# Key/query projection and attention in one block: value projection units inside the first page steps, prompt units merged to 24 in steps 9 to 32

## What is computed

```
kv = rmsnorm(h, kv_norm_w) @ w_kv            # after layer 0: keys, then values, 1024 columns each
q  = rmsnorm(h, norm_mix_w[1]) @ b_w_q       # 8 heads x (2 halves of 64)
# prompt, per head and block of 128 queries, c = 0, 1:
s = einsum(q_c, k_c) * 64**-0.5 - slope * dist      # causal
a = softmax(s[0]) - lam * softmax(s[1]);  o = a @ v
# sample, per sequence: the same over 16 cached pages (through page_table) and the 4 new tokens
def page_step(carry, p):
    kp, vp = cache_k[page_table[:, p]], cache_v[page_table[:, p]]
    s = einsum(qs, kp) + alibi;  return merge(carry, s, vp)
mix = rmsnorm(o, b_subln_w) * (1 - lam_init) @ b_w_o;  h = h + mix;  h = h + hier_moe(rmsnorm(h))
```

## Time and profile before

| | us |
|---|---|
| median of 3 executions | 1745.8 |
| lowest, highest | 1740.0, 1747.0 |
| the profiled execution, whole | 1740.4 |
| its span, first to last instruction | 1738.7 |
| TensorE busy in the span | 1364.6 (78%) |
| VectorE busy | 757.1 (44%) |
| ScalarE busy | 388.2 (22%) |
| bytes moved by DMA | 347.6 MB, 200 GB/s on average |

### The profile page before, as it was taken

The page is one execution under the profiler, slowest core; times in us unless marked ns, Lnnn a source line. Parts: engine busy times, 40 slices in busy tenths (PEclk is TensorE's granted clock), DMA queues, the critical chain, the costliest instruction groups (busy, mean ns, idle before and its releaser), DMA issues. The chain is left out here.

```text
span 1738.7 us, 29140 instructions
## 1 busy us (share of the span) xinstructions
PE 1364.6 (78%) x11207; PEld 790.7 (45%) x11207; DVE 757.1 (44%) x1922; ACT 388.2 (22%) x1062; POOL 170.9 (10%) x242
## 2 busy tenths in 40 slices
PE   3998888887599998908998946666677669999890
PEld 2445555554455655504444434434444325665450
DVE  4205555446665311132101167677777336531115
ACT  2013343333211111102001023333333211021111
POOL 1002222223101000020000011000000000100002
PEclk9998999998699899958998968888888779899995
DMA  5130334113343899830221079999999872589934
GB/s 197 49 127 22 109 105 141 53 61 109 100 174 134 309 371 346 274 122 17 97 100 49 8 236 363 356 367 376 366 357 357 328 244 110 197 299 354 354 101 158
DMA packets 132156, 347.56 MB, mean 200 GB/s; under 512 B 22012, under 2 KB 51887, under 8 KB 123824
## 3 DMA queue, kind: packets, MB, share of 16 engines
q1 hardware_dynamic: 115652, 315.21, 50.4%
q0 software_dynamic: 4992, 17.83, 2.9%
q10 hardware_dynamic: 11372, 12.62, 2.3%
HBM read 302.09 MB, written 43.52 MB: 199 GB/s over the span
## 5 line engine op out<-in xcount | busy, mean ns | idle before, releaser
L404 PE MATMUL bank<-wring,xT 128*128 128x512 f32 x512 | 239.3, 629 | 24.0 <-ACT gla_fin L527 16.1
L2285 DVE STREAM_TRANSPOSE wring<-wring 128x1024 f32<-128x1024 f32 x128 | 154.1, 1225 | 55.4 <-DMA wring<-cache_k 53.8
L404 PEld LDWEIGHTS bank<-wring,xT 128*128 128x128 f32 x512 | 102.0, 202 | 154.2 <-issue 132.9
L2175 PE MATMUL bank<-wring,sa_q 128*32 128x128 f32 x2048 | 89.7, 348 | 100.8 <-DVE sa_red L2294 93.7
L2175 PEld LDWEIGHTS bank<-wring,sa_q 128*32 128x32 f32 x2048 | 78.9, 142 | 110.0 <-issue 100.4
L1304 PE MATMUL bank<-wring,xT 128*128 128x512 f32 x256 | 119.4, 620 | 2.0 <-DVE xT L1224 2.0
L774 PE MATMUL bank<-xT,wring 128*128 128x512 f32 x256 | 111.9, 595 | 0.0
L1304 PEld LDWEIGHTS bank<-wring,xT 128*128 128x128 f32 x256 | 49.3, 199 | 59.4 <-issue 59.3
L682 DVE COPY_PREDICATED gla_att<-level_masks,bank 128x512 f32<-128x512 int32 x48 | 35.0, 730 | 92.6 <-PE bank L794 92.6
L774 PEld LDWEIGHTS bank<-xT,wring 128*128 128x128 f32 x256 | 48.1, 190 | 59.3 <-issue 59.3
L794 PE MATMUL bank<-gla_qe,gla_ke 128*128 128x128 f32 x384 | 52.8, 296 | 4.7 <-DVE gla_att L682 4.7
(11 more groups left out here) (420 smaller groups left out, 2259.3 us busy)
## 6 DMA issues: line engine op xcount, KB each, us to landing
wring<-cache_k SPq DMA_DIRECT2D x128, 512.0 KB, 5.7
wring<-cache_v SPq DMA_DIRECT2D x64, 512.0 KB, 7.3
xT<-cache_v SPq DMA_DIRECT2D x64, 512.0 KB, 6.1
moe_wd<-moe_w_down SPq DMA_DIRECT2D x20, 1024.0 KB, 13.4
wring<-moe_w_gate SPq DMA_DIRECT2D x18, 1024.0 KB, 11.1
wring<-moe_w_up SPq DMA_DIRECT2D x18, 1024.0 KB, 14.2
wring<-a_w_in SPq DMA_DIRECT2D x16, 1024.0 KB, 9.1
moe_wgu<-moe_w_gate SPq DMA_DIRECT2D x14, 1024.0 KB, 10.8
```

The lines of the kernel that those rows point to most:

```text
L404: last = nc.tensor.matmul(bank[:, :], xT[:, c, cols(t)], w[:, c, :], start=(c == 0), stop=(c == DC - 1))
L2175: last = nc.tensor.matmul(out.rearrange("p (r x) -> p r x", r=GROUP), Q[b % 2][:, h, i, :], keys.K[s % 2][:, :, at:at + QUAD], start=(i == ...
L2285: nc.vector.transpose(page, page).then_inc(keys_turned, 1)
```

## The change

1. The two blocks become one. The class Projections holds the instructions of the old projection block without the values; attention_block calls it at the start of each engine's stream. The turning of the keys, one head at a time, now follows each query unit, and the spread of the sample queries follows the third.
2. The ten value units run inside the page steps: two small ones and one large in slot -1, then one large in each of the slots 0 to 6, behind the step's score (value_units_at, V_UNITS). ScalarE copies them out (value_out), where VectorE did.
3. The page buffers change. Keys use a ring tile and the tile that held attn_q_xT. The value pages of the steps 0 to 2 (V_EARLY = 3) share one place, the tile that held the keys (attn_k), since xT and the weights are needed until the last value unit; from step 3 on values have two places as before. K(0) and K(1) are loaded when the queries are done.
4. Prompt units are 24: of each head the blocks 0 and 1 together, then 2, then 3. They start at slot 9 (FIRST = 9). Their tiles lie in the attn_k tile behind the early value pages, so that the table of distances (const_dist) is loaded, and v_prompt stored, in slot 8, when value(2) is done.
5. The load of b_w_o moves from slot 33 to behind the last value pages.
6. In MixOut.tensor, in both layers, gather(0) goes in between the halves of the last projection unit, and gather(2) ahead of norm_turn of the last tile.

```diff
@@ MixOut.tensor
             if i:
                 logits(i - 1)
+            if i == NT - 1:
+                gather(0)
             project(i, 1, w[1], second)
         place(NT - 2)
-        gather(0)
         gather(1)
+        gather(2)
         norm_turn(NT - 1)
         logits(NT - 1)
-        gather(2)
         gather(3)
         place(NT - 1)
@@ CachePages
-        self.K = [by_page(ring[0]), by_page(ring[1])]
-        spare = self.k.xT[:, :, :].rearrange("p c n -> p (c n)")[:, 0:GROUP * D]
-        self.V = [by_page(ring[2]), spare.rearrange("p (r n) -> p r n", r=GROUP)]
+        self.K = [ring[0], by_page(spare)]
+        self.V = [ring[2], by_page(self.k.xT[:, :, :].rearrange("p c n -> p (c n)"))]
+        self.V_early = by_page(early)
+    def values(self, s):
+        return self.V_early if s < V_EARLY else self.V[s % 2]
@@ Projections (was kvq_block)
+    def tensor(self, pe):
...
+        for h in range(HEADS):
+            if h < 2:
+                sample_q(h, w[h])
...
+            last.then_inc(self.q_done, 1)
...
+            turn_k(h)
+            if h == 2:
+                pe.wait_ge(self.qs_out, 2)
+                queries.spread_over_quarters((k.ps[0], k.ps[1]))
+        pe.wait_ge(self.kt_out, 2 * HEADS)
+        queries.new_scores(pe, k.ps[7])
+    def value_unit(self, pe, n):
...
+        if n >= 2:
+            pe.wait_ge(self.v_out, n - 1)
+        project_tokens(self.nc, bank, self.kv_xT, self.w[i], t).then_inc(self.v_done, 1)
+    def value_out(self, act, n):
+        i, t = V_UNITS[n]
+        act.wait_ge(self.v_done, n + 1)
+        for src, part in token_parts(self.k.ps[4 + n % 2], self.v, i, t):
+            last = self.nc.scalar.activation(part, src, ACT.Copy)
+        last.then_inc(self.v_out, 1)
+    def sync(self, sp):
...
+        sp.wait_ge(self.q_done, HEADS)
+        for s in range(2):
+            for r in range(GROUP):
+                keys.load_k(sp, s, r)
+V_UNITS = [(0, PT), (1, PT)] + [(i, t) for i in range(2) for t in range(PT)]
+V_FIRST, V_EARLY = 3, 3
-UNITS = [(h, i) for h in range(HEADS) for i in range(PT)]
-FIRST = 0
+UNITS = [(h, blocks) for h in range(HEADS) for blocks in ((0, 1), (2,), (3,))]
+FIRST = 9
+def value_units_at(s):
+    return range(V_FIRST) if s == -1 else range(V_FIRST + s, min(V_FIRST + s + 1, len(V_UNITS)))
@@ attention_block, SyncE (new order)
+                proj.sync(sp)
+                for s in range(STEPS + LAG):
+                    if 2 <= s < STEPS:
+                        sp.wait_ge(scored, s - 1)
+                        for r in range(GROUP):
+                            keys.load_k(sp, s, r)
...
+                    if s == 2:
...
+                            keys.load_v(sp, 0, r)
+                    v_s = s - LAG
+                    if v_s >= 1:
+                        if v_s >= V_EARLY:
+                            sp.wait_ge(proj.v_done, len(V_UNITS))
+                        if v_s < V_EARLY or v_s >= V_EARLY + 2:
+                            sp.wait_ge(valued, v_s if v_s < V_EARLY else v_s - 1)
+                        for r in range(GROUP):
+                            keys.load_v(sp, v_s, r)
...
+                    if v_s == V_EARLY:
+                        sp.wait_ge(valued, V_EARLY)
+                        sp.dma_start(dist[:, :], a["const_dist"]).then_inc(d_in, 16)
+                        sp.wait_ge(proj.v_out, len(V_UNITS))
+                        proj.store(sp, v, "v_prompt", None, proj.v_stored)
+                sp.wait_ge(scored, STEPS)
+                for i in range(2):
+                    k.load_weights(sp, column_halves(a["b_w_o"][0], i * HB))
@@ attention_block, TensorE and ScalarE
                     if 0 <= s < STEPS:
                         score(s)
+                    for n in value_units_at(s):
+                        proj.value_unit(pe, n)
...
+                    for n in value_units_at(s):
+                        proj.value_out(act, n)
                     if ends is not None:
                         exps(ends)
                         shift_exp(ends)
```

More of the change, by code:

```diff
@@ L1769, in __init__ @@
         self.S_new = sb("scores_new", [P, DEC_B, 2, DEC_T])
-        self.qs, self.kTs = sb("qs", [P, HEADS, SMP]), sb("kTs", [P, HEADS, SMP])
-        self.qz = sb("q_halves", [P, DEC_B, HEADS, QX])
+        n = HEADS * SMP
+        self.qs, self.kTs = (early[:, i * n:(i + 1) * n].rearrange("p (h t) -> p h t", h=HEADS) for i in range(2))
+        self.qz = early[:, 2 * n:4 * n].rearrange("p (b h x) -> p b h x", b=DEC_B, h=HEADS)
         self.rep = sb("q_rep", [P, GROUPS_, HEADS, SMP])
@@ L1857, in __init__, with place @@
         self.v_in = [k.sem(f"sa_v_landed{i}") for i in range(2 * GROUP)]
-    def place(self):
-        by_page = lambda tile: tile[:, :, :].rearrange("p (r c) n -> p r (c n)", r=GROUP)
-        ring = [self.k.wring[(self.k.w_issued + i) % WEIGHT_SLOTS] for i in range(WEIGHT_SLOTS)]
-        self.K = [by_page(ring[0]), by_page(ring[1])]
-        spare = self.k.xT[:, :, :].rearrange("p c n -> p (c n)")[:, 0:GROUP * D]
-        self.V = [by_page(ring[2]), spare.rearrange("p (r n) -> p r n", r=GROUP)]
+    def place(self, spare, early):
+        by_page = lambda flat: flat[:, 0:GROUP * D].rearrange("p (r n) -> p r n", r=GROUP)
+        ring = [by_page(self.k.wring[(self.k.w_issued + i) % WEIGHT_SLOTS][:, :, :].rearrange("p c n -> p (c n)"))
+                for i in range(WEIGHT_SLOTS)]
+        self.K = [ring[0], by_page(spare)]
[3 more added lines that the diff above has]
+        return self.V_early if s < V_EARLY else self.V[s % 2]
     def page(self, sp, s, r):
@@ L2033, in units_at, with parts_of @@
+V_UNITS = [(0, PT), (1, PT)] + [(i, t) for i in range(2) for t in range(PT)]
[4 more added lines that the diff above has]
+    return range(V_FIRST) if s == -1 else range(V_FIRST + s, min(V_FIRST + s + 1, len(V_UNITS)))
+def parts_of(n):
+    h, blocks = UNITS[n]
+    at = 0
+    for x, i in enumerate(blocks):
+        yield x, i, at, (i + 1) * P
+        at = at + (i + 1) * P
 def units_at(s):
@@ L2036, in units_at, with attention_block @@
     return (n,) if 0 <= n < len(UNITS) else ()
-def attention_block(k, a, rep, v, kT, qT, o_s, queries, keys):
+def attention_block(k, a, rep, v, kT, qT, o_s, S, queries, keys, proj):
     nc = k.nc
@@ L2125, in _ @@
                 p_bias_of(1)
-                for b in range(2, DEC_B):
+                for b in range(3, DEC_B):
                     spread_q(b)
-                    p_bias_of(b)
+                    p_bias_of(b - 1)
+                p_bias_of(DEC_B - 1)
                 k.order_n["gpsimd"] = ch.n
@@ L2147, in p_turn @@
                         pe.wait_ge(p_at_out, n)
-                    for j in range(i + 1):
+                    for j in range(sum(i + 1 for i in UNITS[n][1])):
                         last = nc.tensor.transpose(P_TURNED[:, j * P:(j + 1) * P], PS[n % NS][:, 0, j * P:(j + 1) * P], k.ident[:, :])
@@ L2156, in p_values @@
                         pe.wait_ge(p_o_out, n)
-                    for j in range(i + 1):
-                        last = nc.tensor.matmul(P_VALUE[:, 0:P], aT[:, j, :], v[:, j, h * P:(h + 1) * P],
-                                                start=(j == 0), stop=(j == i))
+                    for x, i, at, w in parts_of(n):
+                        for j in range(i + 1):
+                            last = nc.tensor.matmul(P_VALUE[:, x * P:(x + 1) * P], aT[:, at // P + j, :], v[:, j, h * P:(h + 1) * P],
+                                                    start=(j == 0), stop=(j == i))
                     last.then_inc(p_o_done, 1)
@@ L2208, in value @@
                             p = g * GROUP + r
-                            last = nc.tensor.matmul(VALUE[n][QUAD * r:QUAD * (r + 1), :], AT[:, p, :], keys.V[v_s % 2][:, r, n * HB:(n + 1) * HB],
+                            last = nc.tensor.matmul(VALUE[n][QUAD * r:QUAD * (r + 1), :], AT[:, p, :], keys.values(v_s)[:, r, n * HB:(n + 1) * HB],
                                                     start=(g == 0), stop=(g == GROUPS_ - 1 and r > 0))
@@ L2268, in p_bias_max @@
+                        last.then_inc(p_biased, 1)
                     dve.wait_ge(p_biased, 2 * (n + 1))
[L2269 removed]
+                    y = slice(0, len(blocks))
+                    nc.vector.tensor_scalar(s[:, y, 2:4], s[:, y, 0:2], -1.0, None, ALU.mult).then_inc(p_negated, 1)
                 def p_combine(n):
[L2272 to L2274 removed]
@@ L2282, in turn_page @@
+                    last.then_inc(p_combined, 1)
                 def turn_page(s, r):
```

399 lines of the change are left out of this document (186 added, 213 removed).

## The result

The changed kernel takes 1717.9 us (median of 4, 1714.0 to 1718.9), the kernel before beside it 1746.4 us (1740.0 to 1752.4): a ratio of 0.984, 95% interval 0.981 to 0.987. The change gains 28.5 us where 50 were forecast, and the time is 4 us above the end of the range (1714). In the two profiled executions the spans are 1738.7 and 1717.1 us, 21.6 us apart; the profiled execution of before is the shortest of its four.

The account below looks back on a forecast made before the run. TensorE bounds the value projection and the page stream the page steps, one after the other. Terms -52 + 6.5 + 3 - 4.5 - 3.2 = -50.2 us, against the median 1745.8, give 1696 us; range 1681 to 1714.

Parts of the forecast that it names:

- the sum of the start: Up to the issue of K(8): K(8) near 1025 instead of 1077.1, a gain of 52 us (bounds 42 and 60).
- the signs that the prediction named as wrong: Slots 0-6 above 10 us; even score waiting on ScalarE; step over 12 us behind slot 9; K(8) after 1035.
- Rival (a): Start: DMA runs dry, scores of steps 7 and 8 wait, 11.5 to 17 us lost, 1707 to 1713; chance 0.17.
- the softmax wait: Slot 4: TensorE's turn_weights waits for the softmax behind the value unit, 7 us (bounds 0 and 9).
- the 3 that were added: Slot 5, behind slot 4's wait: score and part of a unit at the low clock, 3 us.
- K(8) to K(31): Page stream: 6.5 us for the value store and const_dist plus 3 us for the prompt units' loop.
- The store: Value store (2.1 MB), now in the full page stream: 5.8 us at the stream's rate.
- rival (c): Page stream: prompt units' longer chain, VectorE waiting for ScalarE's exponentials, takes over the loop; 1746 or slower, say 1757; chance 0.02.
- the tail: After K(31): moving b_w_o behind V(31) removes value(28)'s page wait, -4.5 us (bounds -8 and 0).
- the routing: Moved gathers, both layers: last tile's choice 1.6 us earlier each, -3.2 us in all (bounds -7 and +4).
- Rival (b): Page stream gets faster: gaps at DMA share 0.95 filled, 5% of 265 us, 13 us won, 1683; chance 0.10.
- a rule's price: Start: by the skill's clock rule, slots with idle gaps would pay the value unit nearly twice.

Follow-up runs that it names:

- either link: Two runs against the changed kernel: K(7), K(8) issued ahead of V(1), V(2) on SyncE, 1703.0 us; bias_max(2) ahead of step 7's first transpose on VectorE, 1706.8 us.

## Where the prediction was right, and where not

**Wrong: the sum of the start**, by 20.8 of 52 us. The step that failed is the one that gives slot 6 the same 8.9 us as the slots before it, and lets only V(2) wait for the early place. V(1) waits for it too, and it stands ahead of K(7) in SyncE's order. In TensorE's timeline the 20.8 us are score(6)'s wait, 13.3; the low clock of that score and its unit, 3.64 + 7.77 - 1.93 - 7.13 = 2.3; a wait of 2.1 before score(2), which the sum did not have either, with 1.7 for the low clock behind it; and 1.4 in small pieces, the largest 1.1 between the end of value(1) and K(8)'s issue. Of the signs that the prediction named as wrong, two came: slots above 10 us (slot 2 took 12.7, slot 6 24.6) and K(8) after 1035. Cutting either link brought K(8) to 1016.7 and 1027.8, on both sides of the 1025 forecast.

**Rival (a) had the mechanism and a chance of 0.17.** It named the scores of steps 7 and 8; it was score(6), through VectorE's order. Its argument against, that V lands 6 to 7 us behind its issue, took the landing of a first page (6.3 us in the earlier trace rows); a value step needs all four pages, 8.7 us behind the first issue for V(2), 1037.9 to 1046.6. And it counted one landing; the chain has value(0), an issue of V, an issue and a landing of K, a transpose and bias_max in series. Its price of 11.5 to 17 us holds for the chain, 13.3 of waiting and 2.3 of low clock; the time still fell outside its 1707 to 1713, since the start lost 5 us more and the tail and the part behind the block gained nothing. The rule of VectorE's order was in the earlier trace rows, where the prediction uses it for the stream (transpose, then bias_max, then the even score); it was not applied to slot 6.

**Right in the start:** the first K at 924.6 in a block that starts 3.6 us earlier (forecast 929.1 less 3.6), score and unit at 8.9 us in the slots 0, 1, 3 and 4 (slot 2 has the wait above), the softmax wait of 6.7 us (7), and a score of 3.6 us behind it. turn_weights ran at the low clock too, 3.7 us for 1.9; with the score that makes 3.3 us for the 3 that were added.

**Right in size, K(8) to K(31):** +10.7 for +9.5. The store 4.6 for 5.8; the rest, put down to the merged units, 5 for 3. Why it is that much is open. VectorE's waits for ScalarE ahead of p_combine, and so ahead of bias_max, grew from 9.3 to 15.2 us in 220, which is rival (c) in small. But at a DMA share of 1.01 the stretch K(10) to K(31) is still 4 us longer with them (226.3 against 222.2), where the loop no longer binds.

**Wrong, the tail:** 0 to 2 us for 4.5. The wait of value(28) for its pages went, as forecast. The step that failed there is "next late is the copy of the turned weights, at once behind it": that copy is next, but it ends no earlier than the pages had landed before, since the last softmax stands behind the last prompt unit and comes 4.7 us later. V(30), with two places for values, waits for value(28) as it did. b_w_o's place alone changed nothing measurable.

**Too high, the routing:** 1.2 us in layer 0 and 0.1 to 1.0 in layer 1 for 1.6 each, and none of it beyond what these runs can tell.

**A reading that bears on no sum:** the slices at nine tenths in the earlier trace rows are 25 to 31, 1043 to 1347 us, not from 1090 on.

**Rival (b) was half dismissed for a wrong reason.** It said that the stream has 5% in it if the loop is loosened. It has 8 to 9%, 21 of 243 us in the kernel before. The change did not loosen the loop, so the rival did not come true (the loop was the argument against it, and that held). But the prediction also called it impossible by a rule of the Trainium skill (DMA: Bandwidth & Descriptors, Where 436 GB/s comes from), which puts a core's limit from HBM at about 358 GB/s. The trace of this single core has 398 GB/s over 220 us in which nearly all transfers are such pages, and so the measurement decides against that limit here. With the order of VectorE mended in both kernels the change is worth 1711.6 - 1671.2 = 40 us.

## What to carry to other kernels

When stages are laid over each other, write down for every wait that the change adds what stands behind it in its engine's order, and follow each of those to the next order; here a wait of SyncE for a page's place held up a key page, that page a transpose, and the transpose a one-microsecond operation which TensorE needed. A short operation that frees a buffer goes ahead of anything that waits for a transfer. And a resource at a busy share of 0.95 may still be run by a loop: look whether its issues wait for the work that they feed.

## What the runs showed of the hardware

The DMA engines' busy share says little about the rate: at shares of 0.95, 0.96 and 1.01 the same kind of transfer moved 359, 366 and 398 GB/s, 11% more bytes for 6% more share. score(6) ran in 1.93 us where it stood directly behind other matmuls, and in 3.64 us behind its wait of 13.3 us (granted clock 1.00 and 0.50); the value unit behind it then took 7.77 instead of 7.13 us, at a granted clock of 0.91. So a wait cost the short score nearly its length again and the unit 9%, not the double that the prediction set beside its sum as a rule's price.
